# Moving the next chunk's own-value products behind the output products in a chunked delta-rule recursion

## The reference

```python
def step(S, inp):
    r_t, w_t, k_t, v_t, a_t, b_t = inp
    Sa = jnp.einsum("bhvk,bhk->bhv", S, a_t)
    S = S * w_t[:, :, None, :] + Sa[..., None] * b_t[:, :, None, :] + v_t[..., None] * k_t[:, :, None, :]
    y = jnp.einsum("bhvk,bhk->bhv", S, r_t)
    return S, y
```

## Time and profile before

| | |
|---|---|
| median of 3 runs | 956.61 us |
| profiled execution, its own time | 956.54 us |
| its span, first to last instruction | 954.7 us |
| PE busy | 933.7 us, 98% of the span |
| DVE, ACT, POOL busy | 409.4, 428.6, 384.9 us |
| mean granted TensorE clock | 0.997 |
| the recursion's loop, from the L904 of chunk 0 to the end of the L953 of chunk 7 | 344.56 to 383.83 us |

### The profile page before, as it was taken

One profiled execution on the slowest core, in us unless ns is written; L12 is line 12 of the kernel. 1 busy time (PEld: TensorE's weight loads), 2 busy tenths in 40 slices (PEclk: granted clock), 3 DMA queues, 4 the chain that ended last, 5 costly groups with the idle time before them and its releaser, 6 DMA issues.

```text
span 954.7 us, 15908 instructions
## 1 busy us (share of the span) xinstructions
PE 933.7 (98%) x6783; PEld 769.9 (81%) x6783; DVE 409.4 (43%) x645; ACT 428.6 (45%) x683; POOL 384.9 (40%) x180
## 2 busy tenths in 40 slices
PE   6999999999999999999999999999999999999996
PEld 5887888897778778788788888888888888888885
DVE  4223798308565548559244434434344300100435
ACT  6355553235554644623445344443444411412647
POOL 2453444442223526246423444444444444445350
PEclk9999999999999999999999999999999999999998
DMA  7432433332121000226412333333333332323132
GB/s 250 129 92 64 110 88 90 88 90 67 45 59 33 27 25 25 68 71 216 134 44 67 89 106 93 92 107 89 103 96 90 110 110 99 100 89 119 63 105 89
DMA packets 115163, 86.59 MB, mean 91 GB/s; under 512 B 2852, under 2 KB 100022, under 8 KB 115094
## 3 DMA queue, kind: packets, MB, share of 16 engines
q1 hardware_dynamic: 114904, 85.50, 30.3%
q10 hardware_dynamic: 190, 0.08, 0.0%
HBM read 83.47 MB, written 2.10 MB: 90 GB/s over the span
## 4 chain that ended last, share of the span: by engine, by line
PE 95%; ACT 2%; DVE 1%; POOL 1%; DMA 1%; issue 0%; SPq 0%; DVEq 0%
PE bank L544 19%; PE bank L545 18%; PE bank L546 18%; PE bank L606 9%; PE bank L607 9%; PE bank L608 9%; PE bank L863 2%; PE bank L734 1%; PE bank L771 1%; PE bank L819 1%; PE bank L748 1%; POOL w_lo L524 1%; DMA xs<-in_x_dram 1%; PE bank L860 1%; PE bank L904 0%; PE bank L830 0%
## 5 line engine op out<-in xcount | busy, mean ns | idle before, releaser
L524 POOL TENSOR_TENSOR w_lo<-raw,w_hi 128x1024 fp32r<-128x1024 f32 x137 | 330.5, 2412 | 490.4 <-ACT w_hi L1144 490.3
L1144 ACT ACTIVATE w_hi<-raw 128x1024 fp32r<-128x1024 f32 x137 | 145.4, 1061 | 339.6 <-issue 201.2
L544 PE MATMUL bank<-hT_hi,w_hi 128*128 128x512 f32 (+1 forms) x720 | 282.1, 392 | 1.2 <-POOL w_lo L524 1.0
L546 PE MATMUL bank<-hT_hi,w_lo 128*128 128x512 f32 (+1 forms) x720 | 277.0, 385 | 0.0
L545 PE MATMUL bank<-hT_lo,w_hi 128*128 128x512 f32 (+1 forms) x720 | 277.0, 385 | 0.0
L544 PEld LDWEIGHTS bank<-hT_hi,w_hi 128*128 128x128 f32 x720 | 135.2, 188 | 29.3 <-issue 1.7
L546 PEld LDWEIGHTS bank<-hT_hi,w_lo 128*128 128x128 f32 x720 | 135.3, 188 | 27.1
L545 PEld LDWEIGHTS bank<-hT_lo,w_hi 128*128 128x128 f32 x720 | 135.4, 188 | 25.1
L2052 DVE SCALAR_TENSOR_TENSOR cbuf<-bank,params,cbuf 128x511 f32<-128x511 f32 x48 | 36.0, 750 | 132.9 <-ACT cbuf L1542 132.9
L606 PE MATMUL bank<-w_hi,g_hi 128*128 128x512 f32 x184 | 71.7, 390 | 0.0
L608 PE MATMUL bank<-w_hi,g_lo 128*128 128x512 f32 x184 | 71.6, 389 | 0.0
(11 more groups left out here) (318 smaller groups left out, 1350.4 us busy)
## 6 DMA issues: line engine op xcount, KB each, us to landing
raw<-in_w_up_dram SPq DMA_DIRECT2D x48, 512.0 KB, 3.8
raw<-in_w_in_dram SPq DMA_DIRECT2D x33, 512.0 KB, 4.0
raw<-in_w_down_dram SPq DMA_DIRECT2D x24, 512.0 KB, 3.8
raw<-in_w_gate_dram SPq DMA_DIRECT2D x16, 512.0 KB, 4.0
raw<-in_w_out_dram SPq DMA_DIRECT2D x8, 512.0 KB, 4.1
raw<-in_w_ple_gate_dram SPq DMA_DIRECT2D x8, 512.0 KB, 4.2
xs<-in_x_dram SPq DMA_DIRECT2D x4, 512.0 KB, 5.3
raw<-in_w_branch_a_dram SPq DMA_DIRECT2D x4, 512.0 KB, 3.4
```

Of the source, the lines that this page charges most:

```text
L524: nc.gpsimd.tensor_tensor(low(n)[:, :], raw[:, n % RAW_SLOTS, :], high(n)[:, :].bitcast(F32), ALU.subtract).then_inc(*step("pool", ("lo", n)))
L544: nc.tensor.matmul(o, wh, ah, start=first, stop=False)
L546: return nc.tensor.matmul(o, wl, ah, start=False, stop=last)
L1144: nc.scalar.activation(high(u)[:, :], raw[:, u % RAW_SLOTS, :], ACT.Copy) \
```

## The change

`own_values(c + 1)` is issued after `state_and_output(c)` instead of ahead of `solved_u(c)`. Nothing is added or removed, and the other engines' programs stay as they are.

```diff
                 if c in (6, 7):
                     gate_parts(1)
-                if c + 1 < NCH:
-                    own_values(c + 1)
                 if c == 0:
                     gate_parts(2)
                 solved_u(c)
...
                 state_and_output(c)
+                if c + 1 < NCH:
+                    own_values(c + 1)
```

## The result

The changed kernel took 957.88 us in the median of 22 runs, the kernel before 955.44 us in the median of its 22. The ratio is 1.0024, with a 95% interval from 1.0017 to 1.0031: it is slower, by some 2.3 us. I had forecast no difference that can be told, 956.5 us; the kernel got slower instead. That the time lies in my range of 954.4 to 958.4 us is in part luck: the range stood on a median of three runs, 956.61 us, and 22 runs of the same kernel give 955.44.

What follows compares the result with a forecast made beforehand. TensorE, busy 933.7 of 954.7 us, was taken as the bound. Chunk 1's -1.04, x, and 5 (x - 0.46) sum to 6x - 3.34 = -0.04 us, giving 956.5 us from 956.54, range 954.4 to 958.4 us.

Steps and rivals of the forecast that it cites:

- Chunks 2 to 6. Each gains 0.46 us and loses x: Middle chunks: removing L904 ahead of L932 saves 0.46 us, its new place costs x; five times 0.09 us more.
- x: Growth of the stretch from L953 to L918 with L904 put there: 0.55 us, bounds 0.38 to 0.83.
- my sum of -0.04: Whole loop: forecast total change, 6x - 3.34 us, which is -0.04 us with x = 0.55.
- a period above 5.2 us: Sign in chunks 2 and 3: such a period, against 4.83 us forecast, would show the dear wait.
- the dear wait for `pe_own`: Rival at L918: waiting for L904's mark takes 0.96 us, not 0.31; sum +3.9 us, 960.4 us; chance 0.05.
- The larger gap of 0.37 us: Last L953 to L918, taken wholly as a tile-shape drain: x = 0.77 us and 1.3 us more in total.
- Chunks 0 and 1: Loop start: ScalarE's queue moves up, chunk 1's L932 starts at 352.45 and its L819 1.04 us earlier.
- the rival that it would not come forward: ScalarE's copy of u1 in chunk 1 stays at 352.53; sum +0.54, 957.1 us; some 1 in 7 of the 0.91 case.
- a free L904: Rival: the new place behind L953 hides L904 entirely, x = 0; sum -3.3 us, 953.2 us; chance 0.04.

Runs made afterwards that it cites:

- The products twice: Kernel before the change, with L904's products done at the old place and again behind L953; ratio 1.0049.
- The three sets: The changed kernel against the kernel before, run three times with no further edit; ratios 1.0024, 1.0022 and 1.0016.
- the best version: Against the changed kernel, L904 stays behind L953 in chunk 0 but stands directly behind L932 in chunks 1 to 6; ratio 0.9984 to the kernel before, median 953.03 us.

## Why the prediction was right or wrong

**The step that failed** is "Chunks 2 to 6. Each gains 0.46 us and loses x", in its first half. The gain at the old place was 0.46 us only if L819 follows L932 at once. In chunks 2 to 4 it waited for its banks until L932 to L819 took 0.95 us, so the gain was 1.07 - 0.95 = 0.12 us, three times; in chunk 1 the same wait took back 0.83 - 0.61 = 0.22 us, in chunk 5 the gate part started 372.45 - 371.69 = 0.76 us and not 0.61 behind L932. I had asked of each instruction behind L904 what it waits for, the halves of U and the masks, but not of L819 whose bank it writes into. L830's copies were hidden by L904, and I had named no cover for the 0.46 us. Together that is 3 times 0.34 + 0.22 + 0.15 = 1.39 us. With it my sum of -0.04 becomes +1.35; the loop shows +1.33. That it agrees so closely is some luck: x was 0.02 us larger than forecast, six times, and the gain in chunk 1 was 0.10 us larger, and the two cancel.

One of my signs would have misled. I had written that a period above 5.2 us would show the dear wait for `pe_own`; the period came to 5.19 us with an own wait of 0.33 us. It was L819's distance from L932, 0.95 in place of 0.61 us, that told the two apart.

**x was right in kind and size.** It measured 0.57 us (1.36 in place of 0.79 from L953 to L918), against 0.55: 0.15 for the shape (358.68 + 0.42 = 359.10 to 359.25), 0.46 for the records, and 0.33 from L904's last record (359.71) to L918, against 0.31. The products twice gave 0.54 to 0.57 by itself.

The page TensorEngine Tiling of the Trainium skill, Key Properties, has the drain at each change of mode. The trace agrees in kind: with L904 between L948 and L953 three changes of shape cost 0.15 us each with nothing to wait for. The larger gap of 0.37 us, by which I had worked out 1.3 us more, was therefore mostly the wait for the state. That the loop did get 1.3 us longer is a coincidence: the reason is L819's banks.

**Chunks 0 and 1 were right**, but for L819's banks in chunk 1: L932 of chunk 1 started at 351.05 - 343.26 = 7.79 us against the forecast 352.45 - 344.56 = 7.89, as ScalarE's queue came forward as worked out. With that the rival that it would not come forward fell, and those of a free L904 and of a dear own mark fell with x.

**What stays open.** The loop explains 1.33 to 1.57 us. The three sets gave 2.3, 2.1 and 1.5 us; the second and third intervals hold the loop's share, the first begins 0.3 us above 1.33. The hold is ruled out for it. One part of the program behind the loop is known to differ between executions: L606 waits 1.16 us for POOL's w_lo at 457.98 us in the changed kernel, 1.11 before, and in the move in chunks 2 to 4 alone the stretch behind the loop is 562.13 us in one profile and 561.07 in another, in which that wait is missing. It is missing too in the profiles of the best version (561.02 us) and of L904 between L948 and L953 (561.01), and stands in all three of the changed kernel and in the only one of the kernel before. If the changed kernel is spared it less often than the kernel before, that would fill the gap; and if the best version is spared it more often, that would be the second half of its gain. No run here shows how often any of them is spared. The stretch ahead of the loop, the same program in both, is also not told apart from its scatter here, with a single profile of the kernel before.

## What to carry to other kernels

Before you move a group of instructions, list for each one behind its old place not only its data but the buffer that it overwrites, and who still reads it: a filler that fills no hole of its own may be the time in which a bank is emptied. Keep such a filler ahead of the next writer; here it did not need to be ahead of the instruction that is on the chain. And compare two profiles from event to event, since executions of one program differ by more (1.3 us ahead of the loop here) than such a move is worth.

## What the runs showed of the hardware that was not expected

VectorE's square of 128x256, with both operands in SBUF, took 0.41 us alone and 2.58 and 2.59 us when GpSimd's 128x1024 subtraction had started 0.31 us ahead of it; each time it ended 0.28 or 0.29 us after GpSimd's operation. In the changed kernel L1914, which reads PSUM and SBUF, and the reduction L1936, with one operand in SBUF, took 0.43 and 0.42 us beside the same operation. The GPSIMD Engine Reference of the Trainium skill, Specifications, says that GpSimd shares its SBUF interfaces with VectorE and contends with instructions that have two SBUF inputs; the trace agrees, and here it costs the square up to 2.2 us and TensorE 1.3 to 1.9 us, because the next state stands behind it. An idle stretch of 1.92 us of TensorE was followed by half clock for some 6.5 us in one execution, and in another of the same kernel, with an idle stretch of 1.92 us too, the granted clock stayed at 1.00. By the mean granted clock (0.994 or 0.995 against 0.997 to 0.999) it fell in 4 of that kernel's 16 executions.
